# Hybrid decoder step on one core: the first two weight units multiplied side by side, their weights loaded in halves, the constants over ScalarE's queue

## What is computed

```python
h = rmsnorm(x, norm_g)                       # 1024 features
q, f, i, g_a, u, g_b, m_a, m_b = split(h @ w_in)
o, S = hgrn2(silu(q), 1 - fgate, i, log(fgate), s0)      # gated linear recurrence, 4 heads
y_a = (rmsnorm(o) * silu(g_a)) @ w_proj_a
y_b = (pool_mix(u) * pool_scale * silu(g_b)) @ w_proj_b
out = x + (sigmoid(m_a) * y_a + sigmoid(m_b) * y_b) @ w_out
y = rmsnorm(out, final_norm_g)
```

## Time and profile before

| what | us |
|---|---|
| median of 3 runs (1374.23 to 1375.24) | 1374.38 |
| span of the profiled execution, first to last instruction | 1372.1 |
| what lies around the span, median less span | 2.3 |
| TensorE busy in the span | 1359.5 (99%) |
| VectorE busy | 932.0 (68%) |
| ScalarE busy | 685.6 (50%) |
| mean granted TensorE clock | 0.998 |

### The profile page before, as it was taken

One profiled execution on the slowest core, in us unless ns is written; L12 is line 12 of the kernel. 1 busy time (PEld: TensorE's weight loads), 2 busy tenths in 40 slices (PEclk: granted clock), 3 DMA queues, 4 the chain that ended last, 5 costly groups with the idle time before them and its releaser, 6 DMA issues.

```text
span 1372.1 us, 21266 instructions
## 1 busy us (share of the span) xinstructions
PE 1359.5 (99%) x8272; PEld 1345.2 (98%) x8272; DVE 932.0 (68%) x1642; ACT 685.6 (50%) x992; POOL 198.4 (14%) x200
## 2 busy tenths in 40 slices
PE   9999999999999999999999999999999999999997
PEld 7999999999999999999999999999999999999997
DVE  7899655668975456788844567987445689964443
ACT  6565444355664344556643445665433556653332
POOL 2003021110031211001212110012220200130001
PEclk9999999999999999999999999999999999999999
DMA  6544533246535333465363335653532476534338
GB/s 207 140 131 127 208 122 122 94 130 200 143 108 212 118 123 107 129 193 147 98 222 110 121 110 144 171 156 126 189 122 96 136 170 205 178 108 173 118 100 94
DMA packets 140259, 195.91 MB, mean 143 GB/s; under 512 B 83712, under 2 KB 100480, under 8 KB 138496
## 3 DMA queue, kind: packets, MB, share of 16 engines
q1 hardware_dynamic: 140160, 194.56, 47.1%
HBM read 174.91 MB, written 19.61 MB: 142 GB/s over the span
## 4 chain that ended last, share of the span: by engine, by line
PE 92%; DVE 5%; DMA 1%; issue 1%; ACT 1%; SPq 0%; DVEq 0%; ACTq 0%
PE Z L519 29%; PE Z L521 28%; PE Z L520 28%; DVE wlo L1038 1%; DMA wraw<-w_all 1%; PE B L575 1%; PE B L668 1%; PE B L658 1%; PE B L552 0%; DVE xres L1441 0%; DVE snew L1198 0%; DVE h_b L1078 0%; PE B L519 0%; PE B L521 0%; PE B L520 0%
## 5 line engine op out<-in xcount | busy, mean ns | idle before, releaser
L1038 DVE TENSOR_TENSOR wlo<-wraw,whi 128x1024 fp32r<-128x1024 f32 x280 | 367.0, 1311 | 299.7 <-ACT whi L796 299.5
L519 PE MATMUL Z<-hhi,whi 128*128 128x416 f32 x1576 | 552.7, 351 | 0.0
L520 PE MATMUL Z<-hlo,whi 128*128 128x416 f32 x1576 | 549.4, 349 | 0.0
L521 PE MATMUL Z<-hhi,wlo 128*128 128x416 f32 x1576 | 549.4, 349 | 0.0
L796 ACT ACTIVATE whi<-wraw 128x1024 fp32r<-128x1024 f32 x280 | 295.9, 1057 | 425.2 <-PE Z L521 353.0
L519 PEld LDWEIGHTS Z<-hhi,whi 128*128 128x128 f32 x1576 | 296.0, 188 | 0.9 <-issue 0.6
L520 PEld LDWEIGHTS Z<-hlo,whi 128*128 128x128 f32 x1576 | 296.0, 188 | 0.5
L521 PEld LDWEIGHTS Z<-hhi,wlo 128*128 128x128 f32 x1576 | 295.9, 188 | 0.3
L521 PE MATMUL Z<-mhi,wlo 128*128 128x416 f32 x320 | 112.3, 351 | 0.0
L520 PE MATMUL Z<-mlo,whi 128*128 128x416 f32 x320 | 111.9, 350 | 0.0
L519 PE MATMUL Z<-mhi,whi 128*128 128x416 f32 x320 | 111.5, 348 | 0.0
(11 more groups left out here) (252 smaller groups left out, 1555.2 us busy)
## 6 DMA issues: line engine op xcount, KB each, us to landing
wraw<-w_all SPq DMA_DIRECT2D x280, 512.0 KB, 3.5
xres<-xT SPq DMA_DIRECT2D x5, 1664.0 KB, 7.5
xin<-xT SPq DMA_DIRECT2D x4, 1664.0 KB, 7.8
yT<-xres SPq DMA_DIRECT2D x4, 1664.0 KB, 8.9
v_blocks<-h_vt SPq DMA_DIRECT2D x80, 52.0 KB, 3.1
vtm<-v_blocks SPq DMA_DIRECT2D x20, 192.0 KB, 3.9
ktm<-k_blocks SPq DMA_DIRECT2D x20, 192.0 KB, 3.6
k_blocks<-kt SPq DMA_DIRECT2D x64, 52.0 KB, 1.9
```

The source lines that it names most:

```text
L519: pe.matmul(out, wh, xh, start=first, stop=False)
L520: pe.matmul(out, wh, xl, start=False, stop=False)
L521: return pe.matmul(out, wl, xh, start=False, stop=final)
L1038: dve.tensor_tensor(wlo[n % RING][:], raw(t, n)[:], whi[n % RING][:].bitcast(F32), ALU.subtract).then_inc(wlo_made, 1)
```

## The change

Units 0 and 1 are multiplied together (`first_pair`): for each pair of input blocks, first unit 0's matmuls and then unit 1's. For that the weights of both units are loaded, rounded and subtracted in two halves of 512 columns (`LEFT` and `RIGHT`, four input blocks each), with semaphores of their own for the left halves. SyncE issues the halves among the four pieces of the input: piece 0, both left halves, piece 1, unit 0's right half, piece 2, unit 1's right half, piece 3. The load of `cst` goes from SyncE's queue to ScalarE's, ahead of its table load. ScalarE and VectorE work in the order in which the pieces come. In unit 2, `x_squares` stands after all 16 matmuls by `whi` and no longer after 6. Units 2 and on, the warm-up and the rest of the kernel are not touched.

```diff
@@ -292,6 +292,9 @@
         xsq_made, xrs_made, hhi_made = sem("xsq_made"), sem("xrs_made"), sem("hhi_made")
         yhi_made, mhi_made, ysq_made, yrs_made = sem("yhi_made"), sem("mhi_made"), sem("ysq_made"), sem("yrs_made")
         lbe_made = sem("lbe_made")
+        w_half_landed = [sem(f"w_half_landed{i}") for i in range(2)]
+        whi_half_made, wlo_half_made = sem("whi_half_made"), sem("wlo_half_made")
+        LEFT, RIGHT = slice(0, D // 2), slice(D // 2, D)
 
         wlo_made, kin_made, b_made, d_made = sem("wlo_made"), sem("kin_made"), sem("b_made"), sem("d_made")
         q_made, s_made, s0_copied, og_made = sem("q_made"), sem("s_made"), sem("s0_copied"), sem("og_made")
@@ -389,10 +392,10 @@
             for i in range(4):
                 sp.dma_start(xin[:, 2 * i:2 * i + 2, :], xT[0, :, 2 * i:2 * i + 2, :]).then_inc(x0_landed[i], 16)
                 if i == 0:
-                    sp.dma_start(cst[:], consts).then_inc(cst_landed, 16)
-                if i == 0:
-                    sp.dma_start(wraw[0][:], w_all[0]).then_inc(w_landed[0], 16)
-            sp.dma_start(wraw[1][:], w_all[1]).then_inc(w_landed[1], 16)
+                    for n in range(2):
+                        sp.dma_start(wraw[n][:, LEFT], w_all[n, :, LEFT]).then_inc(w_half_landed[n], 16)
+                elif i < 3:
+                    sp.dma_start(wraw[i - 1][:, RIGHT], w_all[i - 1, :, RIGHT]).then_inc(w_landed[i - 1], 16)
             for n in range(RAW, EARLY):
                 sp.dma_start(wraw0[n - RAW][:], w_all[n]).then_inc(w0_landed[n - RAW], 16)
             sp.dma_start(wpl[:], w_pool).then_inc(wpl_landed, 16)
@@ -704,8 +707,8 @@
                     small(t, last, s)
                     if first(t) and s < 3:
                         if s == 0:
-                            first_unit()
-                        else:
+                            first_pair()
+                        elif s == 2:
                             late_low(s)
                         continue
 
@@ -738,39 +741,53 @@
                 if last:
                     y_squares(t, True)
 
-            def first_unit():
-
-                out = Z[0][:, 0:T]
-                pe.wait_ge(whi_made, 1)
-                for k in range(KD):
-                    c = slice(k * P, (k + 1) * P)
+            def first_pair():
+
+                def high(u, k):
+                    pe.wait_ge(whi_half_made if k < KD // 2 else whi_made, u + 1)
                     pe.wait_ge(hhi_made, k + 1)
-                    pe.matmul(out, whi[0][:, c], hhi[k][:], start=(k == 0), stop=False)
+                    pe.matmul(Z[u][:, 0:T], whi[u][:, k * P:(k + 1) * P], hhi[k][:], start=(k == 0), stop=False)
+
+                def low_input(u, k):
                     pe.wait_ge(hlo_made, k + 1)
-                    pe.matmul(out, whi[0][:, c], hlo[k][:], start=False, stop=False)
-                    if k:
-                        first_low(out, k - 1, False)
-                first_low(out, KD - 1, True).then_inc(acc_done, 1)
+                    pe.matmul(Z[u][:, 0:T], whi[u][:, k * P:(k + 1) * P], hlo[k][:], start=False, stop=False)
+
+                def low_weights(u, k):
+                    pe.wait_ge(wlo_half_made if k < KD // 2 else wlo_made, u + 1)
+                    return pe.matmul(Z[u][:, 0:T], wlo[u][:, k * P:(k + 1) * P], hhi[k][:], start=False,
+                                     stop=(k == KD - 1))
+
+                for k in range(0, KD, 2):
+                    if k == 2:
+                        for i in (k, k + 1):
+                            for u in range(2):
+                                high(u, i)
+                                low_weights(u, i)
+                            for u in range(2):
+                                low_input(u, i)
+                        continue
+                    for u in range(2):
+                        for i in (k, k + 1):
+                            high(u, i)
+                            low_input(u, i)
+                        for i in (k, k + 1):
+                            mm = low_weights(u, i)
+                        if k == KD - 2:
+                            mm.then_inc(acc_done, 1)
 
             def late_low(u):
 
                 out = Z[u][:, 0:T]
                 pe.wait_ge(whi_made, u + 1)
                 for k in range(KD):
-                    if u == 2 and k == 3:
-                        x_squares()
                     c = slice(k * P, (k + 1) * P)
                     pe.matmul(out, whi[u][:, c], hhi[k][:], start=(k == 0), stop=False)
                     pe.matmul(out, whi[u][:, c], hlo[k][:], start=False, stop=False)
+                x_squares()
                 pe.wait_ge(wlo_made, u + 1)
                 for k in range(KD):
                     mm = pe.matmul(out, wlo[u][:, k * P:(k + 1) * P], hhi[k][:], start=False, stop=(k == KD - 1))
                 mm.then_inc(acc_done, 1)
-
-            def first_low(out, k, final):
-                if k == 0:
-                    pe.wait_ge(wlo_made, 1)
-                return pe.matmul(out, wlo[0][:, k * P:(k + 1) * P], hhi[k][:], start=False, stop=final)
 
             def x_squares():
 
@@ -990,6 +1007,7 @@
                     act.wait_ge(yacc_made, nth(t, KD - 1, j - 3))
                 act.activation(yacc[:] if j == 0 else ysq[j % 2][:], xres[:, j, :], ACT.Square).then_inc(ysq_made, 1)
 
+            act.dma_start(cst[:], consts).then_inc(cst_landed, 16)
             act.preload_act_table_set(LN_EXP)
             act.wait_ge(zeroed, ZEROED)
             act.wait_ge(cst_landed, 16)
@@ -1002,15 +1020,23 @@
             def square(k):
                 act.activation(h0[k][:], xin[:, k, :], ACT.Square).then_inc(xsq_made, 1)
 
+            def split_half(n, c, landed, made):
+                act.wait_ge(landed[n], 16)
+                act.activation(whi[n][:, c], wraw[n][:, c], ACT.Copy).then_inc(made, 1)
+
             weighted_hi(0)
             weighted_hi(1)
+            split_half(0, LEFT, w_half_landed, whi_half_made)
+            split_half(1, LEFT, w_half_landed, whi_half_made)
             square(0)
-            split(0, 0)
             weighted_hi(2)
             weighted_hi(3)
-            for k in range(4, KD):
-                weighted_hi(k)
-            split(0, 1)
+            split_half(0, RIGHT, w_landed, whi_made)
+            weighted_hi(4)
+            weighted_hi(5)
+            split_half(1, RIGHT, w_landed, whi_made)
+            weighted_hi(6)
+            weighted_hi(7)
             square(1)
             split(0, 2)
             for k in range(2, KD):
@@ -1498,14 +1524,22 @@
                 dve.wait_ge(rc_used, G)
                 dve.reciprocal(rc[:], rc[:]).then_inc(rc_used, 1)
 
+            def split_half(n, c, hi_made, made):
+                dve.wait_ge(hi_made, n + 1)
+                dve.tensor_tensor(wlo[n][:, c], wraw[n][:, c], whi[n][:, c].bitcast(F32), ALU.subtract).then_inc(made, 1)
+
             weighted_lo(0)
             weighted_lo(1)
-            split(0, 0)
+            split_half(0, LEFT, whi_half_made, wlo_half_made)
+            split_half(1, LEFT, whi_half_made, wlo_half_made)
             weighted_lo(2)
             weighted_lo(3)
-            for k in range(4, KD):
-                weighted_lo(k)
-            split(0, 1)
+            split_half(0, RIGHT, whi_made, wlo_made)
+            weighted_lo(4)
+            weighted_lo(5)
+            split_half(1, RIGHT, whi_made, wlo_made)
+            weighted_lo(6)
+            weighted_lo(7)
             split(0, 2)
             for k in range(2, KD):
                 dve.wait_ge(xsq_made, k + 1)
```

## The result

The changed kernel takes 1376.31 us (median, 1375.04 to 1377.23), the kernel before, timed beside it, 1374.23 (1373.25 to 1375.24): a ratio of 1.0015, interval 1.0009 to 1.0021. That is 2.1 us slower, where 0.1 was forecast, and above the range. The profiled execution of the changed kernel has a span of 1374.5 us, 2.4 more than the kernel before's.

The account below looks back on a forecast made before the run. TensorE, busy throughout from 23.55 us, was taken to set the end. 0.8 us won at the start, 0.8 given back at line 658 and 0.1 lost by the chain gave 1374.5 us, range 1373.2 to 1375.8.

Parts of the forecast that it names:

- The pair: Units 0 and 1 on TensorE: begins near 7.9 us, operands about 1 us to spare, no wait, unit 2 from 16.8.
- the warm-up covers the earlier `whi`: Start of TensorE: the warm-up occupies it until some 7.8 us, so the earlier first weights were costed at nothing.
- the lead: TensorE at unit 2's start: 0.8 us ahead of the kernel before, at 16.8 instead of 17.66.
- full pace from the first paired matmul: Units 0 and 1 on TensorE: all matmuls expected at the 2.4 GHz pace, 0.186 us each.
- Nothing, but with no cover left: Unit 2's later sums of squares: `xrs0` ready at 22.6 us, 0.2 before VectorE comes to it, so no cost.
- the whole chain: VectorE's and ScalarE's work from the first scaling to `at_sb` before line 658: expected 0.1 us later.
- The rival of a late `xrs0`: First scaling: if the pair gained nothing, `xrs0` ready at 23.43 us, the chain 0.8 behind, 1375.2; chance 0.12.
- What the lead meets: Line 658, head 0's outputs: TensorE spends its 0.8 us waiting for `at_sb`, then goes on 0.1 us later than before.
- from there on the order of things is the old one: Behind line 658: the order is unchanged, so the shift of 0.1 us stays to the end.
- The signs named beforehand: Profile checks: among them, wrong if VectorE idles for `xrs0` or line 658's place comes near 51.5; expected near 52.4.
- The upper bound of the chain's shift, +1.0: VectorE's and ScalarE's chain: slowest bound given for its shift; the fastest was -0.9.
- The rule that I weighed: DMA loads: about 2.0 us fixed plus bytes at 436 GB/s; four halves 10.4 us, two wholes 6.4, time 1378.5.

Follow-up runs that it names:

- e4: Changed kernel with the load of the constants back on SyncE's queue, behind the first input piece: 1375.96 us (ratio 1.0016).
- e7: Changed kernel with the sums of squares early and the small loads first for keys and values of all heads and tiles: 1374.70 us (1.0004).
- e13: Changed kernel with the sums of squares early and 3 instead of 4 warm-up matmuls: 1374.06 us (1.0002).
- e14: Changed kernel with the sums of squares early and 2 instead of 4 warm-up matmuls: 1373.41 us (0.9997).
- e1: Changed kernel with the sums of squares back after 6 matmuls of unit 2: 1374.20 us (1.0002).
- e3: Changed kernel with ten redundant matmuls on TensorE ahead of head 0's wait for the keys in tile 0: 1374.58 us (1.0004).
- e5: Changed kernel with the 16 KB key load of head 0, tile 0 issued ahead of the 192 KB one: 1376.12 us (1.0014).
- e15: Changed kernel with 3 instead of 4 warm-up matmuls and nothing else: 1375.92 us (1.0013).
- e12: Kernel before with 3 instead of 4 warm-up matmuls and 20 small matmuls behind them: 1374.57 us (1.0005).
- e6: Changed kernel with the sums of squares early and head 0, tile 0's 16 KB key load ahead of the 192 KB one: 1374.33 us (1.0002).
- e10: Changed kernel with 3 instead of 4 warm-up matmuls and 20 small matmuls behind them: 1373.81 us (1.0001).
- e16: Changed kernel with the sums of squares early, 2 warm-up matmuls and 36 small matmuls: 1374.11 us (0.9999).
- e8: Changed kernel with 6 instead of 4 warm-up matmuls: 1375.63 us (1.0011).
- e9: Kernel before with 6 small matmuls behind the warm-up on TensorE: 1373.94 us, no difference.

## Why the prediction was wrong

**The pair.** Right: no wait for operands, every load in time, the warm-up covers the earlier `whi`. Mis-sized: the lead was 0.38 us instead of 0.8, since the clock rose at 8.7 us and not before the pair began: its rise is not tied to the end of the warm-up. I had read "full pace from the first paired matmul" out of one profile. In the variants the pair starts between 6.22 and 8.07, its first matmuls at the slow pace in some profiles (after, e4, e7, e13, e14) and at the full pace from the first in others (e1, e3, e5, e15).

**`xrs0`.** "Nothing, but with no cover left" was read rightly and cost wrongly. With the lead smaller by 0.4 us than forecast, `xrs0` came at 23.1 and the whole chain 0.5 us late. The rival of a late `xrs0` had this mechanism, with 0.12 and up to 0.8 us.

**What the lead meets.** This is the step that failed: "from there on the order of things is the old one", with line 658 as the one place where TensorE meets the chain. The chain also ends in a transfer: stores and loads of keys, for a product six microseconds ahead of line 658. In the kernel before, the keys are there at 46.2 and TensorE comes at 46.74: 0.5 us of slack that I never looked up, since no wait stood there. The chain's 0.5 us uses it up, and the load took 1.8 us longer, so the product came 1.8 us late, and with its lead of 0.4 TensorE stood 2.1 us. Neither the forecast nor a rival had this wait. The signs named beforehand did show it was off: VectorE idled for `xrs0`, and line 658's place came at 55.60. The upper bound of the chain's shift, +1.0, has no sum behind it; the rival that it points to gives 0.8.

**Why the load took longer.** Not the halves (e12 has none of them), not the constants' queue (e4), not the order of the key loads (e5, e6). Moving the load of instructions by TensorE fillers takes the slow landing away from the changed kernel (e10, e16) and brings it to the kernel before (e12). That a key load lands 1.5 to 2 us later when this packet comes ahead of its last packets is shown. That it does so by holding one of the 16 DMA engines is my reading: the remaining key packets start as the packet ends and then come one by one, but the records do not name the engine.

**The clock.** Not in the prediction at all: I spoke of it only at the start. It is 1.5 us of the profiled loss at line 661. e8 has the wait of the changed kernel without the fall and a span 1.6 us shorter; e1 against e15 gives 1.5; e3 fills the wait and keeps the clock, but its chain was also earlier. How the 2.1 us of the medians divide between the wait and the fall is not shown, since the fall comes in some executions only.

**The rule that I weighed.** The Trainium skill's page DMA: Bandwidth & Descriptors (sections Bandwidth and Anatomy of one DMA) would, by the estimate made from it, have put four halves 4.0 us above two wholes, at 1378.5. By the rows the pair had no wait for a half; the time, 1376.31, lies between that figure and mine (1374.5), for a reason unrelated to it.

**Still open.** Where the packet of instructions comes is not explained by a count of instructions: 36 more move it by 7 us in the changed kernel (e10) and by 0.9 in the kernel before (e12), and 12 more by 0.1 (e9). Nor was it tried whether e14's 0.6 us would stand in more runs. And why the clock falls behind the wait in one execution and not in the next is not told by these traces.

## What to carry to other kernels

Follow a moved piece to every meeting of the engines behind it, transfers included, and write down the slack at each: where no wait stands, the profile does not tell how near it is, and both times have to be looked up. A lead on one engine is worth nothing while another chain sets the next meeting, and the longer wait can cost a second time, by the clock behind it; filler work in such a wait is cheap. When a small load lands late for no reason of its own queue, look at the other queues at that time, instruction loads among them.

## What the runs showed of the hardware

Instructions are loaded in packets of 16 KB, 66 of them in the changed kernel. The one near 45.7 us took 1.0 us (after) and 1.4 us (before). The profile page's row of their queue, packets, MB and share of 16 engines:

```profile
q8 instruction: 66, 1.08, 0.3%
```

A change of a few instructions shifts these packets against the kernel's own transfers: a key load of 16 KB took 3.5 to 3.7 or 5.0 to 5.5 us, and four stores took 1.88, 2.74 or 3.60 us to issue.

TensorE's granted clock fell to 0.50 at or behind waits of 3.3 us (e5), 3.0 (e15) and 2.2 (after), and did not behind 2.2 (e8), 2.1 (e1), 2.0 (e6) and 1.8 (e4); in the changed kernel it stayed there for 3.4 us. At the start the granted column stands at 1.00 while the warm-up and, in some executions, the pair's first matmuls run at the pace of 1.2 GHz, in e14 until 10.5 us. The column says nothing there: the trace's own records of the clock begin only at 8.67 us (after) and 10.48 (e14).
